# Memory attention, latent attention and the output projection in one stage over blocks of 512 queries, with q, k and v split before they go to DRAM

## The reference

```python
h = rms_norm(x, g_attn);  proj = h @ w_in        # 1376 columns for three groups of heads
out_a = swa_sink_attention(...)                  # 8 window heads, d = 64
qb = (rms_norm(mq_a) @ w_uq)                     # latent heads: 4, q and k of 96, v of 64
kv = (rms_norm(mkv_a) @ w_ukv)
out_b = mla_attention(qb, kb, vb)                # chunk-causal over 2048 keys
km, vm = split(rms_norm(mem) @ mem_w_kv)         # 4 memory heads, 256 keys, d = 64
out_m = memory_attention(qm, km, vm)
x = x + concat(out_a, out_b, out_m) @ w_o        # 1024 x 1024
hf = rms_norm(x, g_ffn)
x = x + square(relu(hf @ w_ff1)) @ w_ff2         # 4096 hidden features
```

## Time and profile before

| | us |
|---|---|
| median of 3 runs | 2449.18 |
| lowest, highest | 2446.03, 2465.76 |
| the profiled execution, its own time | 2458.1 |
| its span | 2456.3 |
| busy in it: PE, DVE, ACT, POOL | 2258.6, 1424.3, 1017.8, 1145.9 |

### The profile page before, as it was taken

The page is one execution under the profiler, slowest core; times in us unless marked ns, Lnnn a source line. Parts: engine busy times, 40 slices in busy tenths (PEclk is TensorE's granted clock), DMA queues, the critical chain, the costliest instruction groups (busy, mean ns, idle before and its releaser), DMA issues. The chain is left out here.

```text
span 2456.3 us, 31729 instructions
## 1 busy us (share of the span) xinstructions
PE 2258.6 (92%) x10376; PEld 1865.6 (76%) x10376; DVE 1424.3 (58%) x1972; ACT 1017.8 (41%) x1726; POOL 1145.9 (47%) x944
## 2 busy tenths in 40 slices
PE   4899999959888987999599998999999989999999
PEld 3788889845567765887488886888878768888887
DVE  4466666656756764243676678777664454443543
ACT  4454555434467775222433334433332322223221
POOL 1354454436678884052566556656635740002211
PEclk8999899967799998999799999999999999999999
DMA  5122222131221112554554447445447764233463
GB/s 191 48 54 51 53 54 61 33 114 36 57 53 33 23 42 99 154 180 154 187 169 153 141 147 255 142 143 164 163 170 269 247 235 146 87 123 115 157 214 112
DMA packets 252807, 308.79 MB, mean 126 GB/s; under 512 B 46767, under 2 KB 168303, under 8 KB 250382
## 3 DMA queue, kind: packets, MB, share of 16 engines
q1 hardware_dynamic: 251534, 303.04, 38.3%
q10 hardware_dynamic: 1152, 4.19, 0.5%
HBM read 201.66 MB, written 105.51 MB: 125 GB/s over the span
## 5 line engine op out<-in xcount | busy, mean ns | idle before, releaser
L310 PE MATMUL f_bank<-f_t_hi,f_w_hi 128*128 128x512 f32 x896 | 352.7, 394 | 35.1 <-DVE f_t_lo L2021 23.0
L310 PE MATMUL f_bank<-f_w_hi,f_a_hi 128*128 128x512 f32 x896 | 350.9, 392 | 13.9 <-DVE f_y L2057 8.1
L310 PE MATMUL f_bank<-f_t_lo,f_w_hi 128*128 128x512 f32 x896 | 351.7, 393 | 0.0
L310 PE MATMUL f_bank<-f_t_hi,f_w_lo 128*128 128x512 f32 x896 | 351.3, 392 | 0.0
L310 PE MATMUL f_bank<-f_w_lo,f_a_hi 128*128 128x512 f32 x896 | 350.6, 391 | 0.0
L310 PE MATMUL f_bank<-f_w_hi,f_a_lo 128*128 128x512 f32 x896 | 350.5, 391 | 0.0
L1232 POOL TENSOR_TENSOR a_p_lo<-a_prob,a_p_hi 128x512 fp32r<-128x512 f32 x192 | 230.0, 1206 | 86.2 <-issue 21.6
L310 PEld LDWEIGHTS f_bank<-f_t_hi,f_w_hi 128*128 128x128 f32 x896 | 169.8, 190 | 74.4 <-issue 31.4
L2036 DVE TENSOR_TENSOR f_a_lo<-f_a_raw,f_a_hi 128x1024 fp32r<-128x1024 f32 x112 | 162.3, 1449 | 90.1 <-ACT f_a_hi L1964 89.8
L1926 POOL TENSOR_TENSOR f_r<-f_r,f_y 128x512 f32<-128x512 f32 x24 | 42.0, 1786 | 362.0 <-DMA f_r<-s_x 362.0
L310 PEld LDWEIGHTS f_bank<-f_w_hi,f_a_hi 128*128 128x128 f32 x896 | 169.3, 189 | 50.8 <-issue 13.3
(11 more groups left out here) (280 smaller groups left out, 5084.8 us busy)
## 6 DMA issues: line engine op xcount, KB each, us to landing
f_a_raw<-s_aop SPq DMA_DIRECT2D x112, 512.0 KB, 4.5
w_raw<-in_w_ff SPq DMA_DIRECT2D x64, 512.0 KB, 5.4
s_aop<-f_a SPq DMA_DIRECT2D x128, 256.0 KB, 2.6
s_aop<-f_s SPq DMA_DIRECT2D x96, 256.0 KB, 2.4
f_w_raw<-in_w_ff SPq DMA_DIRECT2D x64, 256.0 KB, 5.6
f_t_raw<-s_hop SPq DMA_DIRECT2D x14, 1024.0 KB, 6.2
f_r<-in_w_ff SPq DMA_DIRECT2D x48, 256.0 KB, 5.7
p_x<-in_x SPq DMA_DIRECT2D x16, 512.0 KB, 4.4
```

What stands on the lines that cost most here:

```text
L310: ins = pe.matmul(out, a, b, start=(first and j == 0), stop=(last and j == n - 1))
```

## The change

`attend` and `project_out` become one stage, `attend_and_project`. Its outer loop is over the four blocks of 512 queries, its inner loop over the eight heads, a memory head and a latent head in turn (2 and 4, 8, 12 or 16 steps). q, k and v are split where they are made, in the first two stages, and stored as two parts, with the additional rows of ones and zeros stored once; attention loads them ready for TensorE, k and v in pieces of 512 keys into rings of three. The store of the sums and their reload, and the same for the shares, stand in different slots. w_o is loaded on SyncE's queue and split during the first block. Its products for a block are dealt out over the slots in which the next block's attention runs, in portions of three products (256 in all); those of the last block come after the last step. The window heads' output is loaded tile by tile. The norm's scaling is on ScalarE, the gain after the transposes on VectorE, the tiles are paired 2n and 2n + 1. Banks of PSUM: `pS` 2 (3 before), `pX` for turns and transposes, `pY` one for w_o, and `pA` beside it in the last four tiles. The loads of w1 go to the start of the MLP. In `front` the rotary product works in place.

```diff
+                v = kv[:, :, MH * MD:].rearrange("p b (h d) -> p b h d", d=MD)
+                ac.activation(v_out[:, :, :, 0, :], v, ACT.Copy).then_inc(v_hi_done, 1)
...
+                for b in range(NMT):
+                    dve.wait_ge(act, step(5, b))
+                    dve.tensor_tensor(k_lo[:, :, b * P:(b + 1) * P], pT[b][:, :, :], k_hi[:, :, b * P:(b + 1) * P].bitcast(F32),
+                                      ALU.subtract).then_inc(k_lo_done, 1)
...
+                wait(sp, rows_made, 2)
+                for one, dst in ((0, S["k_mla"][0, LD]), (1, S["k_mla"][1, LD]), (1, S["q_mla"][1, LD]), (1, S["q_mem"][1, MD])):
+                    sp.dma_start(dst.rearrange("h (a t) -> (h a) t", t=SEQ * LH // P), rows[:, one, :].bitcast(F32)).then_inc(rows_stored, 16)
+                for one, dst in ((0, S["k_mem"][0, MD]), (1, S["k_mem"][1, MD])):
+                    sp.dma_start(dst.rearrange("h (a t) -> (h a) t", t=NMEM * MH // P), rows[:, one, 0:NMEM * MH // P].bitcast(F32)).then_inc(rows_stored, 16)
...
-                        wait(sp, m_staged, t.n + 1)
-                        sp.dma_start(S["q_mem"][:, :, span(t)], stage_m[:, :, :]).then_inc(m_stored, 16)
+                        wait(sp, m_hi_done, t.n + 1)
+                        sp.dma_start(S["q_mem"][0, 0:MD, :, span(t)], m_hi[:, :, :].bitcast(F32)).then_inc(m_stored, 16)
+                        wait(sp, m_lo_done, t.n + 1)
+                        sp.dma_start(S["q_mem"][1, 0:MD, :, span(t)], m_lo[:, :, :].bitcast(F32)).then_inc(m_stored, 16)
...
+                        wait(pool, lv_hi_done, t.n + 1)
+                        wait(pool, l_act, t.n * L_ACT + 3)
+                        pool.tensor_tensor(lv[:, :, 1, :], lkv[:, :, LN:], lv[:, :, 0, :].bitcast(F32), ALU.subtract).then_inc(lv_lo_done, 1)
...
+                        wait(ac, lv_stored, 16 * t.n)
+                        ac.activation(lv[:, :, 0, :], up_kv[:, :, LN:], ACT.Copy).then_inc(lv_hi_done, 1)
...
+                        wait(dve, m_hi_done, t.n + 1)
+                        dve.tensor_tensor(m_lo[:, :, :], pB[0:MD, :].rearrange("p (h q) -> p h q", q=P), m_hi[:, :, :].bitcast(F32),
+                                          ALU.subtract).then_inc(m_lo_done, 1)
+                    if live(tr, NT):
+
+                        t = tr
+                        for j, src in enumerate((pC[0:LD, :], pD[0:LD, 0:LH * P])):
+                            wait(dve, l_hi_done, t.n * 2 + 1 + j)
+                            dve.tensor_tensor(l_lo[j][:, :, :], src.rearrange("p (h q) -> p h q", q=P), l_hi[j][:, :, :].bitcast(F32),
+                                              ALU.subtract).then_inc(l_lo_done, 1)
...
-    R32, RP, RS = 4, 5, 3
...
+    LAG, GAP = 4, 4
+    R32, RP, RS = 3, 5, 2
+    RQ, RL, RF, RB = 5, 2, 4, 2
+    KP, KR, VR = 3, 3, 3
+    HC = DM // 2
+    PER = 2 * KD
...
+    for u in range(NU):
+        for hd in heads:
+            n = QT * (u + 1) if hd["causal"] else NMEM // P
+            U = len(units)
+            units.append(dict(hd=hd, u=u, start=len(steps), n=n, chunks=[], piece=len(pieces)))
             for k in range(n):
                 d0 = k * P - u * UQ if hd["causal"] else -1
-                steps.append((len(units) - 1, k, min(max(d0, 0), UQ - 256), d0))
...
+            put("sum_back", end + 2, U)
             put("invert", end + 4, U)
-        put("scale", end + 9 if U + 1 < len(units) else end, U)
-    at_k_split = -1000
-    for h, hd in enumerate(heads):
-        need = chunk_slot[units[h * NU]["chunks"][0]] - 1
-        number = -(-hd["nkeys"] // (PIECE * P))
+        put("kp_load", max(chunk_slot[chunk_first[n]] - 8, chunk_slot[chunk_last[n - KP]] + 1 if n >= KP else -1000), n)
+        put("k_load", max(piece_first[n] - 9, piece_last[n - KR] + 1 if n >= KR else -1000), n)
+        put("v_load", max(piece_first[n] + LAG - 9, piece_last[n - VR] + LAG + 1 if n >= VR else -1000), n)
+    for k in range(KD):
+        put("wo_load", 3 * k - (8 if k < 2 else 5), k)
+        put("wo_split", 3 * k, k)
...
+    ready = [scale_slot[8 * (u + 1) - 1] + 4 for u in range(NU)]
+    portion_slot = []
+    for u in range(NU):
+        for i in range(QT * PER):
+            if u + 1 < NU:
+                portion_slot.append(ready[u] + i * (ready[u + 1] - ready[u]) // (QT * PER))
+            else:
+                portion_slot.append(max(ready[u], portion_slot[-1]) + (i % 4 == 0 and i > 0))
...
+            return [pY, pA[0], pA[1]][(2 * t + a) % 3] if t >= NT - QT else pY
+
+        def y_free(t, a):
+
+            n = 2 * t + a
+            return max((m for m in range(n) if y_bank(m // 2, m % 2) is y_bank(t, a)), default=-1) + 1
...
+                    for n in of("k_load", s):
+                        U, j, w = pieces[n]
+                        hd, b = units[U]["hd"], n % KR
+                        wait(sp, qk_done, piece_last[n - KR] + 1 if n >= KR else 0)
+                        for e, k in enumerate((k_hi, k_lo)):
+                            sp.dma_start(k[b][0:hd["D"] + 1, 0:w].bitcast(F32), S[hd["k"]][e, 0:hd["D"] + 1, hd["h"], j * CW:j * CW + w]).then_inc(k_loaded[b], 16)
+                    for n in of("v_load", s):
+                        U, j, w = pieces[n]
+                        hd, b, T = units[U]["hd"], n % VR, CW // P
+                        if n < VR:
+                            sp.wait_ge(filled, 2 * (n + 1))
+                        wait(sp, pv_done, piece_last[n - VR] + 1 if n >= VR else 0)
+                        for e in range(2):
+                            sp.dma_start(v[b][:, e, 0:w // P, 0:VD].bitcast(F32), S[hd["v"]][j * T:j * T + w // P, :, hd["h"], e, :].rearrange("t p d -> p t d")
+                                         ).then_inc(v_loaded[b], 16)
...
+                    for U in of("sum_back", s):
                         sp.wait_ge(sum_out, 16 * (U + 1))
-                        sp.dma_start(sums[b][:, :], S["sums"][U, :].rearrange("(p n) -> p n", n=QT)).then_inc(back[b], 16)
-                    for U in of("invert", s):
-
-                        b = U % RF
-                        wait(sp, inverted, U + 1)
-                        sp.dma_start(S["shares"][U, :].rearrange("(p n) -> p n", n=QT), sums[b][:, :]).then_inc(share_out, 16)
+                        sp.dma_start(sums[U % RF][:, :], S["sums"][U, :].rearrange("(p n) -> p n", n=QT)).then_inc(back[U % RF], 16)
+                    for U in of("share_back", s):
                         sp.wait_ge(share_out, 16 * (U + 1))
                         wait(sp, scaled, U - RB + 1)
...
+                    for t, a in of("added", s):
+                        dve.wait_ge(y_made, 2 * t + a + 1)
+                        dve.wait_ge(x_loaded[t % 2], 16 * (t // 2 + 1))
+                        half = x2[t % 2][:, a * HC:(a + 1) * HC]
+                        dve.tensor_tensor(half, y_bank(t, a)[:, :], half, ALU.add).then_inc(added, 1)
...
+                    for t, a, k in of("portion", s):
+                        b = t % 2
+                        if k == 0:
+                            pe.wait_ge(m_lo_done, 2 * t + 2)
+                            wait(pe, added, y_free(t, a))
+                            if t == 0:
+                                pe.wait_ge(w_lo_done, KD)
+                        ins = products(pe, y_bank(t, a)[:, :], [(m_hi[b][:, k, :], m_lo[b][:, k, :], w_hi[:, k, a * HC:(a + 1) * HC], w_lo[:, k, a * HC:(a + 1) * HC])],
+                                       first=(k == 0), last=(k == KD - 1))
+                        if k == KD - 1:
+                            ins.then_inc(y_made, 1)
+                    for t, e in of("turn_h", s):
...
+                    if j == 1:
+                        load_w1(sp, F, 0, 0, 0)
                     if j >= 2:
                         wait(sp, t_loaded[j - 2], 16)
                     load_t(0, j)
```

More of the change, by code:

```diff
@@ L547, in _ @@
                 wait(pool, const_made, FILLS)
+                for one in range(2):
+                    pool.memset(rows[:, one, :].bitcast(F32), 1.0 - one).then_inc(rows_made, 1)
+                    wait(pool, rows_made, one + 1)
                 def prepare():
@@ L1031, in attend @@
-    at = {name: {} for name in ("chunk", "turn", "q", "q_load", "k", "v", "k_load", "v_load", "stage", "invert", "scale")}
+                steps.append((U, k, min(max(d0, 0), UQ - 256), d0))
+            number = u + 1 if hd["causal"] else 1
+            for j in range(number):
+                pieces.append((U, j, CW if hd["causal"] else NMEM))
+            for ch in range(number):
+                for q in range(QT):
+                    keys = (QT * u + q + 1) * P if hd["causal"] else NMEM
+                    units[-1]["chunks"].append(len(chunks))
+                    chunks.append((U, q, ch, min(CW, keys - ch * CW)))
@@ new lines, in attend_and_project, with piece_at, end_of @@
+    N, NUNITS = len(steps), len(units)
+    def piece_at(U, k):
+        return units[U]["piece"] + k // (CW // P)
+    def end_of(U):
```

(40 more changed lines are left out.)

754 lines of the change are left out of this document (323 added, 431 removed).

## The result

| | us |
|---|---|
| before, median of 4 runs (lowest, highest) | 2452.3 (2446.03, 2465.76) |
| after, median of 4 runs (lowest, highest) | 2992.38 (2989.99, 2997.09) |
| ratio, with its 95% interval | 1.2196 (1.2141 to 1.2251) |
| span of the profiled execution, before and after | 2456.3, 2990.9 |
| busy after: PE, DVE, ACT, POOL | 2328.1, 1402.0, 989.8, 1069.8 |

The change makes the kernel 22% slower where 2% faster was forecast: a clear miss, and far outside the range. The work is the same: PE has 10376 products before and after, and VectorE, ScalarE and GpSimd are busy for less time than before. So the 535 us are waits and the slow clock that comes with them.

A forecast was written before the change was run, and what follows sets the result against it. The rebuilt stage held 487 us of TensorE work in 656, the rest waits and low clock. Terms sum to 596.5 against 655.6: 59 less, minus 15 added before it, 44; 2458.1 becomes 2414, median scale 2405; range 2345 to 2455.

The forecast's parts named there:

- before the stage, more than before: Ahead of the rebuilt stage: memory stage +5, front's start +6, front tiles 0, last three tiles +4; together 15 us.
- first load to slot 0: Start of rebuilt stage, until its first step of 128 keys for 512 queries: 14 us, bounds 9 and 20.
- slots 0 to 24: First query block, four pairs of memory and latent units, VectorE needing most: 72 us, bounds 57 and 87.
- slots 24 to 41: Attention steps still without w_o portions: 32 us, at 1.9 us a slot.
- slots 41 to 200: Attention with w_o portions between, chains covered by other products: 395 us including 3% for imperfection, bounds 383 and 440.
- gap and tail of w_o: After attention's last product: 5 us idle, then 48 us of 64 portions and 32 transposes with nothing beside them.
- last chain and the MLP's start: Stage's end: last tile's chain from addition to store 17 us, then MLP's start 13.5 us.
- the queue's price: SyncE's queue in the stage: 581 transfers at 0.58 us each, 337 us in under 600, fitting on the mean.
- The load queue becomes the bound: Waits on SyncE's in-order queue hold later loads; 56 pieces each 1.6 us late, +90 us, 2495 us; chance 0.11.
- the clock doesn't come: Stage keeps clock 0.94 rather than 1.00: +28 us and 10 of stalls, 2443 us; chance 0.14, shared with unit chain.
- Packs better: Stage's first block at its busiest engine's pace, fewer losses elsewhere: 45 us more gain, 2360 us; chance 0.20.
- it does not do what it says: TensorE meets the maxima, turn, row chain at each of 32 units: +48 us, 2453 us; chance within the clock's 0.14.

The follow-up runs named there:

- the second kernel: Changed kernel with the latent heads' constant row set once in the ring buffers by VectorE and 96 partitions loaded: 2458.48 us, ratio to before 1.001.
- experiment 2: Kernel before plus a prologue of single loads of R rows, 2 KB each: 9.56 us a load for 97 rows, 2.34 for 96.
- mended kernel: Same as the second kernel: the changed kernel with every latent load on 96 partitions, 2458.48 us.

## Why the prediction was wrong

The same terms, with what each took in the profiled execution. The marks are the first load on SP, and then TensorE's: first score product, step 24, step 41, end of the last product of values, end of the last product of w_o, first product of the MLP.

| term, us | predicted | after | 96 partitions | best kernel |
|---|---|---|---|---|
| before the stage, more than before | 15 | 8.3 | 7.0 | 6.9 |
| first load to slot 0 | 14 | 10.8 | 12.2 | 16.7 |
| slots 0 to 24 | 72 | 136.5 | 69.8 | 64.7 |
| slots 24 to 41 | 32 | 111.6 | 49.6 | 43.0 |
| slots 41 to 200 | 395 | 831.8 | 428.1 | 405.7 |
| gap and tail of w_o | 53 | 54.8 | 55.1 | 56.3 |
| last chain and the MLP's start | 30.5 | 32.8 | 32.8 | 33.2 |
| stage | 596.5 | 1178.3 | 647.7 | 619.6 |

**The step that failed** is the queue's price: "I count 581 transfers in the stage ... At 0.58 us each that is 337 us of queue in under 600, so it fits on the mean." The count was not the matter: the second kernel has the same 581. The 0.58 us come from one load of 96 partitions, and I put them on 96 loads that the change makes one row longer. Alone, such a load takes 9.56 us in place of 2.34, on one DMA engine. A queue priced by issues alone had no term for the engine behind it. The added row stood in the diff, in the slice of each load, and I costed "the additional rows" only where they are stored, at the front's start. 96 times 8.2 us is 790 us against the 499 us that I had for all 200 slots, and these took 1080. That price is experiment 2's; no row of before had it. The Trainium skill's rule named above would have given one engine for 97 rows, and I didn't hold it against these loads.

**The rivals.** "The load queue becomes the bound" was right in kind, and its mark in the trace came: score products that wait for DMA, for q_lo above all (173.1 us). Its reason was another, loads held behind a late wait of SP, and it had 1.6 us of lateness a piece, 90 us, where 580 us were lost over the slots. Its argument against itself was the landing of 512 KB in 4.5 us, again a transfer of a harmless number of partitions. The clock (0.58 to 0.77) followed the stalls and wasn't the cause of the 530 us: with 96 partitions it is back at 0.96 over slots 41 on. "Packs better" came in no kernel. The other two rivals can't be judged in the kernel after, but in the mended one they are near: it took 2458 us, where "the clock doesn't come" had 2443 and "it does not do what it says" 2453. Its clock over attention is 0.91, not near 1.00, and TensorE waits 29.4 us for the maxima.

**What held.** The small runs of the values were costed at nothing beyond their issue, and that held: 3.5 us to land with 96 partitions. Front tiles at 0: the steady part has 396.84 us of products in 400 us, and from TensorE's start (81.40 us instead of 76.37, 5 later, the lower end of the 5 to 12 named) to the last product of the front's projection (486.91 instead of 483.17) it is even 1.3 us shorter. So the additions ahead of the tail cost 3.7 us, where I had 11; the rows of ones and zeros are issued in 2.8 us, from 54.90, while other things are still awaited. The front's tail added 4.6, where I had 4. The gap, the tail and the MLP's start are within 3 us.

The first block took 69.8 us in the mended kernel, where I had 72, the middle between 57 and 87 for want of a better row. That is partly luck: the sign that was to go with it, VectorE busy over 80%, did not come (44.0 of 69.9 us, 63%), and the clock was 0.72.

**What was off even without the 97 partitions**, by 51 us of stage: slots 24 to 41 (17.6 too small) and the steady part (33, inside its bounds of 383 to 440). Over slots 24 to 41 the mended kernel's clock was 0.76, and TensorE stood 5.8 us for q_lo with its two buffers, which my list of shorter rings left out. With the third buffer the stretch took 43.4 us at a clock of 0.88; what makes up the other 11 us is open. In the steady part the cover by other products held for the score banks, but not for the maxima, and the clock of 0.96 in place of 1.00 is by my own 378 us of products some 16 of the 33 us, an estimate. In the profiled executions the third buffer gave back 11 us of this stretch (428.1 to 416.8), and the burst rate as much again: 3% for all imperfection was too little. The best kernel, with a third buffer for q_lo and the slower rate, is worth 19 us in the same runs (2440.34 against 2459.77), not the 44 that I had. One sum of the working is loose: 224 maximum products of 393 columns are some 40 us by the pitch of 0.23 us for 512, not 43; nothing above hangs on it.

## What to carry to other kernels

Price a transfer by how it spreads over the DMA engines, not by its bytes or its issue alone: when a change alters the number of partitions of a load, compare the new number's divisors with the old one's. One row added to 96 turned a load of 2.34 us into one of 9.56. A constant row can be set once in the buffer, or loaded by itself: both gave back all of the loss, and their times (2458.48 and 2460.57 us) are not told apart. The mark in a profile is issues of several us on the queue, beside long waits for loads, while the DMA engines are on the average little busy. The share alone says nothing: in attention it was 0.16 to 0.20 in the kernel before, 0.26 in the kernel after and 0.57 in the mended one. And the long issue is not always the guilty one, but often what stands behind it.

When one bound is removed, measure the next before counting the whole gain: here three kernels that relieved the queue gave some 4 us at most, and a change of two numbers in the planner gave 11.

## What was not expected of the hardware

The time of a load against its number of partitions, with 2 KB a row: 2.34 us for 96, 9.56 for 97, 2.30 for 98, 12.09 for 127, 3.42 for 95. And that the backlog reaches the issuing queue: SP spent up to 10.8 us on a single issue of k_lo, where the median for the same load with 96 partitions is 0.43, and VectorE waited up to 33.3 us for a transfer of 2 KB that has nothing to do with these loads, most of it because SP came to issue it so late.
